# A further arm for experts with at most 32 tokens: 32 columns, two gate/up units in one pass of four column tiles

## The reference

```
logits = (h @ router)
probs = softmax(logits)
vals, idx = top_k(probs, 2)          # 256 tokens, 8 experts
combine = one_hot(idx) * vals / sum(vals)
for e in range(8):                   # w_gate[e], w_up[e]: 1024 x 3584, w_down[e]: 3584 x 1024
    out = out + combine[..., e] * ((silu(h @ w_gate[e]) * (h @ w_up[e])) @ w_down[e])
```

## Time and profile before

| | |
|---|---|
| median of 3 runs (lowest, highest) | 1636.34 us (1633.12, 1638.41) |
| the profiled execution's own time | 1634.14 us |
| its span, first to last instruction | 1632.4 us |
| TensorE matmul busy | 1524.1 us, 93% of the span |
| VectorE, ScalarE busy | 381.2 us (23%), 266.3 us (16%) |
| mean granted TensorE clock | 0.968 of 2.4 GHz |
| moved by DMA | 474.35 MB, mean 291 GB/s |

### The profile page before, as it was taken

The page is one execution under the profiler, slowest core; times in us unless marked ns, Lnnn a source line. Parts: engine busy times, 40 slices in busy tenths (PEclk is TensorE's granted clock), DMA queues, the critical chain, the costliest instruction groups (busy, mean ns, idle before and its releaser), DMA issues.

```text
span 1632.4 us, 22184 instructions
## 1 busy us (share of the span) xinstructions
PE 1524.1 (93%) x9552; PEld 980.6 (60%) x9553; DVE 381.2 (23%) x663; ACT 266.3 (16%) x506; POOL 16.6 (1%) x18
## 2 busy tenths in 40 slices
PE   5999999999999799799879999996999998999897
PEld 3445598864686464454369954545995564553462
DVE  2668514400265421110010100211010120110212
ACT  3235210001100222121100001221000131120122
POOL 1000010000000000000000000000000000000000
PEclk7999999999999799899989999998999999999999
DMA  9863176842687269889827766798878699889595
GB/s 388 339 255 139 71 291 253 301 187 82 253 316 302 108 283 426 375 339 373 371 75 262 274 244 232 303 428 358 295 287 303 243 428 427 358 350 407 227 428 243
DMA packets 34239, 474.35 MB, mean 291 GB/s; under 512 B 3824, under 2 KB 4112, under 8 KB 5696
## 3 DMA queue, kind: packets, MB, share of 16 engines
q1 hardware_dynamic: 32800, 467.90, 72.2%
q0 software_dynamic: 1024, 3.38, 0.6%
q10 hardware_dynamic: 288, 1.05, 0.2%
HBM read 471.26 MB, written 1.05 MB: 289 GB/s over the span
## 4 chain that ended last, share of the span: by engine, by line
PE 84%; DMA 7%; issue 4%; DVE 4%; ACT 1%; SPq 0%; DVEq 0%
PE ps L1204 22%; PE ps L1186 13%; PE ps L1242 13%; PE ps L997 9%; PE ps L974 8%; DMA ring<-stream 7%; PE ps L1048 5%; PE ps L1135 4%; PE ps L843 3%; PE ps L1260 2%; PE ps L1174 1%; DVE acc L511 1%; DVE att L574 1%; PE ps L945 0%; PE ps L1219 0%
## 5 line engine op out<-in xcount | busy, mean ns | idle before, releaser
L1204 PE MATMUL ps<-ring,hTe 128*64 128x256 f32 (+1 forms) x3584 | 361.8, 384 | 11.3 <-issue 9.9
L1204 PEld LDWEIGHTS ps<-ring,hTe 128*64 128x64 f32 (+1 forms) x3584 | 216.6, 131 | 134.4 <-issue 27.3
L1242 PE MATMUL ps<-ring,aT 128*64 128x512 f32 (+2 forms) x1232 | 286.7, 597 | 7.9 <-DMA ring<-stream 6.4
L1186 PE MATMUL ps<-hTe,ring 128*128 128x144 f32 (+1 forms) x1792 | 215.2, 284 | 20.9 <-issue 20.9
L1186 PEld LDWEIGHTS ps<-hTe,ring 128*128 128x128 f32 x1792 | 214.6, 194 | 22.7 <-issue 22.7
L1242 PEld LDWEIGHTS ps<-ring,aT 128*64 128x64 f32 (+2 forms) x1232 | 96.2, 139 | 188.0 <-issue 170.7
L760 DVE TENSOR_TENSOR aT<-hT,ps 128x512 f32<-128x512 f32 x112 | 77.0, 687 | 548.0 <-ACT hT L419 548.0
L419 ACT ACTIVATE hT<-ps 128x512 f32<-128x512 f32 x112 | 66.9, 597 | 569.5 <-PE ps L1204 337.1
L997 PE MATMUL ps<-hT,ring 128*128 128x256 f32 (+1 forms) x832 | 153.4, 347 | 0.0
L997 PEld LDWEIGHTS ps<-hT,ring 128*128 128x128 f32 x832 | 138.1, 191 | 15.7 <-issue 1.0
L511 DVE SCALAR_TENSOR_TENSOR acc<-ring,silu_c,acc 128x1024 f32<-128x1024 f32 (+1 forms) x92 | 105.2, 1143 | 2.0
(11 more groups left out here) (180 smaller groups left out, 705.1 us busy)
## 6 DMA issues: line engine op xcount, KB each, us to landing
ring<-stream SPq DMA_DIRECT2D x222, 2048.0 KB, 11.1
gg<-norm_w POOLq DMA_DIRECT2D x4, 512.0 KB, 14.8
x<-x_in SPq DMA_DIRECT2D x1, 1024.0 KB, 5.1
hTe<-ctx_in SPq DMA_DIRECT2D x1, 1024.0 KB, 7.9
out<-x ACTq DMA_DIRECT2D x2, 512.0 KB, 2.6
aT<-dft POOLq DMA_DIRECT2D x1, 512.0 KB, 10.8
aT<-rope POOLq DMA_DIRECT2D x1, 256.0 KB, 15.4
acc<-late POOLq DMA_DIRECT2D x1, 192.0 KB, 2.7
```

Of the source, the lines that this page charges most:

```text
L1186: last = pe.matmul(ps[:, 2 * (u % 2) + b, g * SEQ:g * SEQ + width], w, hTe[:, k, 0:width], start=(k == 0), stop=(k == KD - 1))
L1204: last = pe.matmul(to, hTe[:, k, s0:s0 + n], w, start=(k == 0), stop=(k == KD - 1))
L1242: last = pe.matmul(ps[n * r:n * (r + 1), 4 + 2 * b + h, :], a_T, w[:, f, h * BANK:(h + 1) * BANK], start=(j < tiles), stop=(j >= NFE - tiles))
```

## The change

There is a new first class, 32, with an arm of its own ahead of the others. In it the even units do no products. An odd unit does its own and the even one's in one pass: four column tiles of 32, two for the unit before and two for this one. Counting semaphores then go up by two, and one transpose serves two units. Slots are freed in pairs, by the first matmuls of the next pass. Down uses four tiles of 32. By the token counts above, experts 0 and 3 use this arm; the other six use the arms they used before.

```diff
-WIDTHS = (64, 96, 128, 144, 160, 192, 256)
-WIDE = 2
+WIDTHS = (32, 64, 96, 128, 144, 160, 192, 256)
+WIDE = 3
-BLOCKS = {64: [(0, 64)], 96: [(0, 64), (64, 32)], 128: [(0, 128)], 144: [(0, 128), (128, 32)],
+BLOCKS = {32: [(0, 32)], 64: [(0, 64)], 96: [(0, 64), (64, 32)], 128: [(0, 128)], 144: [(0, 128), (128, 32)],
...
                 def done_before(width, u):
+                    if width == 32 and u < GU_UNITS:
+                        return [u - 3, u - 2] if u % 2 and u > 1 else []
...
                 def turn(width, u):
+                    if width == 32 and u % 2 == 0:
+                        return
                     pe.wait_ge(e_a, e * GU_UNITS + u + 1)
...
-                    last.then_inc(eT_ps, 1)
+                    last.then_inc(eT_ps, 2 if width == 32 else 1)
                 def gate_up(width):
                     for u in range(GU_UNITS):
                         landed_of(e, u)
+                        if width == 32 and u % 2 == 0:
+                            continue
...
-                        last.then_inc(e_ps, 1)
+                        last.then_inc(e_ps, 2 if width == 32 else 1)
                         if u == 1:
                             pe.wait_ge(comb_ok, e * 4 + 4)
-                        if u and not is_wide(width):
+                        if width == 32:
+                            if u > 1:
+                                turn(width, u - 2)
+                        elif u and not is_wide(width):
                             turn(width, u - 1)
```

## The result

The changed kernel takes 1682.22 us (median), against 1635.12 us for the kernel before in the same runs: a ratio of 1.0284, 95% interval 1.0264 to 1.0304, 47.1 us slower. It was forecast at 1674, between 1657 and 1688. The profiled executions, on which all that follows rests, have spans of 1680.3 and 1632.4 us: 47.9 apart.

The account below looks back on a forecast made before the run. TensorE holds 84% of the chain, but DMA loads were taken to set expert 0's end and branches the gaps between experts. Terms 2.6 + 28.3 + 1.4 + 5.3 + 0.2 = 37.8 us gave 1674, range 1657 to 1688.

Parts of the forecast that it names:

- The halved passes: Experts 0 and 3: some 29 us less TensorE time in each, counted at nothing because DMA covers it.
- The wait between passes: Experts 0 and 3: first loads issued by the second pass, so each ends 1.3 us later; +2.6 us.
- One more arm to skip: Before experts 1, 2, 4, 5, 6 and 7: one more dear branch each, over an arm's code; +28.3 us.
- The combine's chain: In the combine: one more short branch of 0.24 us, six times; +1.4 us, nothing if hidden.
- The clock: Lower TensorE clock after gaps: slower starts of experts 5 and 6, slower gathers behind 0 and 3; +5.3 us.
- skips are free: Rival: each conditional branch over an arm costs 0.25 us, so 28.3 becomes 1.5; 1647 us, chance 0.04.
- Partly resident: Rival: two or three skips find their target code still held and are cheap; about 1660 us, chance 0.10.
- The arm's clock: Rival: gaps between passes put the new arm at half clock, +8 us per expert; 1690 us, chance 0.07.

Follow-up runs that it names:

- x8: Changed kernel with each gate/up matmul of the new arm moving half of its columns, as many instructions; 1678.61 us, ratio 1.0270.
- x5: Changed kernel with each even unit's slot freed by the last matmul of its own pass, not the first of the next; 1675.67 us, ratio 1.0259.
- x1: Changed kernel with the first comparison always true, so the new arm stands in the program but is never run; 1692.61 us, ratio 1.0351.
- x2: Kernel before with one more branch ahead of the arms, over a never-run arm holding a single wait; 1636.68 us, ratio 1.0005.
- x3: Changed kernel with the new arm tested and placed behind those of 64, 96, 128 and 144; 1693.53 us in one run.
- x4: Changed kernel with half of the contraction of gate/up left out in the new arm, 448 fewer instructions; 1659.42 us, ratio 1.0158.
- both trees: Chain of branches made a tree, in the changed kernel (1662.81 us, ratio 1.0174) and in the kernel before (1622.26 us, ratio 0.9922).

## Why the prediction was right, point by point

**The halved passes are worth nothing.** Shown. The change itself took some 21 us of TensorE's gate/up products out of expert 0, and its last load landed 1.1 us later behind the expert's start, not earlier. With half of the columns the kernel gained only what an earlier first load gives (x8). The last unit's products didn't even become shorter in expert 0: 3.62 us at the lower clock, where x8, at another clock there, has 1.92. In both, the jump out of the arm covers it.

**The wait between passes, +2.6.** The mechanism is shown by x5; the size was low. The second pass began 5.7 us behind the first, and the first load was issued 6.4 us behind the start of expert 0, not 5.6. The last landing of experts 0 and 3 moved by 1.1 and 2.5 us, together 3.6, 1.0 above the term.

**One more arm to skip, +28.3.** The mechanism is shown by x1 and x2, the places by x3. The number of dear branches came out as forecast, one more ahead of each of the six. The term was too small by 8.1; issue ahead of the arms grew by 36.4. Three things made up most of it. Expert 2's four skips took 19.1 us where three took 13.1, 6 more instead of 4.7. Expert 4's second took 7.53, dearer than any row of before. And the loop-end jumps ahead of experts 2 and 7 rose, from 3.3 and 3.4 to 5.1 and 4.7 us; I had looked only at the chain, not at how far everything behind the arms moves. The traces show what these two waited for: each has one 16 KB packet of code within it before and two in the changed kernel. That adding or taking code in an arm changes which jumps are dear is shown by x4; why these two now need a second packet is not shown.

**The combine's chain, +1.4.** The branches are there at about 0.23 us, and the combine follows the gather with no gap: hidden, 0.

**The clock, +5.3.** Expert 5's first two units took 9.16 us instead of 7.13, +2.0 for 2.7 forecast; expert 6's first piece +0.7 for 1.0. The gathers grew by 3.2, for 1.6, and the largest of it, 1.7, was behind expert 2, where I had none: the gap there grew from 1.83 to 2.33 us, and the gather took 8.86 instead of 7.17. Behind expert 0, where I had +0.8, the gap was no longer (2.79 us, 3.07 before) and the gather stayed at 8.86.

**Not forecast**: 2.8 us behind expert 7's products, and 1.3 us ahead of expert 0, whose cause stays open. Of the 2.8, 1.1 is a later start of the last combine, behind a jump out of the arm of 5.09 us instead of 3.40 (again two packets of code instead of one), and 1.7 the combine itself: 5.40 us instead of 3.71, at a clock of 0.72 in 1665 to 1671 against 1.00.

**The sum.** It came out 10 us low (37.8 against 47.9), 8.1 of it in the skips. The forecast holds because its range was wide enough for that, not because errors cancelled: the only term clearly too large was the combine's, by 1.4.

**The rivals.** That skips are free, at 0.25 us each, fell in the first rows, and is right only for near targets (0.24 us in x2). The Trainium skill's page "Advanced Engine Details and Errata", section Control Flow Timing, gives about 108 ns for a compare-and-branch; the taken ones here are above it even where they are near, and those that fall through are at 0.06 to 0.10 us. "Partly resident" occurred in none of the skips that I had priced as dear in the changed kernel, but it is what made x4 and both trees faster than I expected: it was the right mechanism with too little weight in my expectations. The arm's clock fell in part (0.77 in 607 to 659), but the loads covered it.

## What to carry to other kernels

A branch over a long unrolled body can wait for a load of code: 3.7 to 5.2 us for such a skip in the changed kernel with idle DMA, 6.1 to 7.5 us while the ring was being refilled. And every rare case put ahead of the common ones is paid by all of them. Before adding a special arm, ask what sets the end of the cases that would use it: here the loads did, and halving the passes was worth nothing. When an experiment takes work out, keep the number of instructions the same, or the run measures the code's length too, and read from the trace how much busy time really went. And where many arms must be, a tree whose neighbours run after each other costs less than a chain; here it and a hint for the loop made the kernel before 1.3% faster.

## What the runs showed of the hardware that I had not expected

- The length of an arm's code decides a jump elsewhere: 7.26 or 0.23 us for the same jump at the loop's end, with 448 instructions less in between.
- The price of a far branch goes with the packets of code that it waits for: 3.34 us with one and 5.11 with two for the same jump at the loop's end ahead of expert 2, both with DMA otherwise idle.
- In expert 0, TensorE at half of the columns with the same gaps went to its lower clock in the second pass (0.50 in 584 to 587) and took 3.61 us for half the work, where the changed kernel had 1.00 over 580 to 608. Less work in a pass was no faster there. In expert 3 the difference is smaller: with half of the columns the second pass took 1.95 us and the third 3.53, and in the changed kernel the third took 5.01.
- A gap of 2.33 us was followed by a gather of 8.86 us (clock 0.57 in 1028 to 1032), while one of 1.83 before left it at 7.17. The gap alone doesn't decide it: the 2.35 us ahead of expert 5 in the kernel before left the clock at 1.00. The first of these:

```profile
1028.00:1032.00 4.00, 3.88 (x10) 3.15 (x11) 0.00 (x0) 0.25 (x1) 0.00 (x0) 0.57 0.41 86
```
